# Making the inputs of a linear recurrence inside a top-k selection stage, per group of heads, and passing them through memory

## What is computed

```python
ps = p[..., :N_SHIFT]
ps = ps + (token_shift(ps) - ps) * shift_mu[l]
...
w_log = -jax.nn.softplus(-(w0 + jnp.tanh(pwd) @ w2).astype(f32)) - 0.5
decay = jnp.exp(-jnp.exp(w_log))
a = jax.nn.sigmoid((a0 + pad_ @ a2).astype(f32))
kk = heads(pk * k_k)
kk = kk / jnp.maximum(jnp.sqrt(jnp.sum(kk * kk, axis=-1, keepdims=True)), 1e-12)
k = pk.astype(f32) * (1.0 + (a - 1.0) * k_a)
...
y = rwkv7_scan(r_h, w_h, k_h, v_h, -kk, kk * a_h)
...
bonus = jnp.sum(r_h * k_h * r_k.astype(f32), axis=-1, keepdims=True) * v_h
```

## Time and profile before

| what | us |
| --- | --- |
| median of 3 runs (2827.34 to 2830.3) | 2829.26 |
| the profiled execution, its own time | 2830.62 |
| its span, first to last instruction | 2828.8 |
| TensorE busy in the span | 2563.4 (91%) |
| VectorE | 1502.1 (53%) |
| GpSimd | 901.7 (32%) |
| ScalarE | 784.5 (28%) |

### The profile page before, as it was taken

One profiled execution on the slowest core, in us unless ns is written; L12 is line 12 of the kernel. 1 busy time (PEld: TensorE's weight loads), 2 busy tenths in 40 slices (PEclk: granted clock), 3 DMA queues, 4 the chain that ended last, 5 costly groups with the idle time before them and its releaser, 6 DMA issues. The chain is left out here.

```text
span 2828.8 us, 40567 instructions
## 1 busy us (share of the span) xinstructions
PE 2563.4 (91%) x17201; PEld 2090.3 (74%) x17201; DVE 1502.1 (53%) x2111; ACT 784.5 (28%) x1334; POOL 901.7 (32%) x475
## 2 busy tenths in 40 slices
PE   7998899999999999989899999999898316899997
PEld 5887788888888888868675788887676106888686
DVE  5113633442422212234866899994565696555943
ACT  4205443310111101234424222211553311111332
POOL 3212333442433424444431122221310522111664
PEclk9999999999999999999999999999999658999999
DMA  3113212222221111122340133322100002100523
GB/s 132 40 37 121 74 45 104 68 80 90 80 90 63 45 45 52 45 82 75 102 152 30 60 105 90 105 89 78 64 1 21 14 30 77 33 4 9 197 91 109
DMA packets 76084, 200.06 MB, mean 71 GB/s; under 512 B 8408, under 2 KB 13056, under 8 KB 75904
## 3 DMA queue, kind: packets, MB, share of 16 engines
q1 hardware_dynamic: 65248, 178.06, 19.6%
q10 hardware_dynamic: 10656, 19.40, 1.8%
HBM read 166.88 MB, written 31.60 MB: 70 GB/s over the span
## 5 line engine op out<-in xcount | busy, mean ns | idle before, releaser
L339 PE MATMUL ps<-region_rounded,weights_hi_by_slot 128*128 128x512 f32 x2432 | 958.9, 394 | 32.9 <-DVE region_rounded L617 14.1
L340 PE MATMUL ps<-region_rounded,weights_hi_by_slot 128*128 128x512 f32 x2432 | 951.3, 391 | 0.0
L341 PE MATMUL ps<-region_rounded,weights_lo_in_place 128*128 128x512 f32 x2432 | 951.1, 391 | 0.0
L333 POOL TENSOR_TENSOR weights_lo_in_place<-wbuf,weights_hi_by_slot 128x1024 fp32r<-128x1024 f32 x194 | 486.2, 2509 | 933.9 <-ACT weights_hi_by_slot L329 933.9
L339 PEld LDWEIGHTS ps<-region_rounded,weights_hi_by_slot 128*128 128x128 f32 x2432 | 460.1, 189 | 135.0 <-issue 30.5
L340 PEld LDWEIGHTS ps<-region_rounded,weights_hi_by_slot 128*128 128x128 f32 x2432 | 459.8, 189 | 97.2 <-issue 2.6
L341 PEld LDWEIGHTS ps<-region_rounded,weights_lo_in_place 128*128 128x128 f32 x2432 | 459.4, 189 | 96.6
L329 ACT CAST weights_hi_by_slot<-wbuf 128x1024 fp32r<-128x1024 f32 x194 | 202.0, 1045 | 356.9 <-DMA wbuf<-w_mlp 218.9
L1819 DVE MAX8 gcols<-region 128x8 f32<-128x384 f32 (+5 forms) x192 | 171.7, 894 | 6.7 <-PEq L1708 0.3
L1821 DVE MATCH_REPLACE8 region<-gcols,region 128x384 f32<-128x384 f32 (+5 forms) x192 | 168.1, 876 | 0.0
L1529 DVE TENSOR_TENSOR region<-ps,region 128x512 f32<-128x512 f32 x64 | 44.1, 689 | 215.2 <-PE ps L341 215.1
(11 more groups left out here) (334 smaller groups left out, 3499.8 us busy)
## 6 DMA issues: line engine op xcount, KB each, us to landing
wbuf<-w_mlp SPq DMA_DIRECT2D x64, 512.0 KB, 3.6
wbuf<-w_hn SPq DMA_DIRECT2D x37, 512.0 KB, 4.7
scratch_hn_out<-tmp ACTq DMA_DIRECT2D x74, 256.0 KB, 4.8
region<-scratch_hn_out SPq DMA_DIRECT2D x37, 512.0 KB, 7.5
wbuf<-w_in SPq DMA_DIRECT2D x25, 512.0 KB, 3.7
region<-xT SPq DMA_DIRECT2D x24, 512.0 KB, 6.8
xtra<-w_ada SPq DMA_DIRECT2D x32, 384.0 KB, 4.2
wbuf<-w_att SPq DMA_DIRECT2D x20, 512.0 KB, 3.6
```

What stands on the lines that cost most here:

```text
L333: self.nc.gpsimd.tensor_tensor(self.m.lo4[:, n % SLOTS, :], self.m.raw4[:, n % SLOTS, :], self.m.hi4[:, n % SLOTS, :].bitcast(F32), ALU.su ...
L339: nc.tensor.matmul(out, m.hi4[:, s, w], m.rounded(hi + k, half(hf)), start=(k == 0), stop=False)
L340: nc.tensor.matmul(out, m.hi4[:, s, w], m.rounded(lo + k, half(hf)), start=False, stop=False)
L341: return nc.tensor.matmul(out, m.lo4[:, s, w], m.rounded(hi + k, half(hf)), start=False, stop=(k == KT - 1))
```

## The change

The selection stage's 37 units are put in another order (`HN_ORDER`): first the low rank unit (12), then for each group p its k, r and v unit and five other units, then the rest. So a group's period is 16 halves (`PERIOD`), and `group_at(j, first)` names the group whose step `first` falls on half j: j = 3 + first + 16p. At fixed steps each engine has a piece of one group's work behind its own:

- ScalarE drains a mixed unit twice per half, scaled by 1 - mu and by mu (the latter one column to the right, into xtra), and GpSimd adds the two (`mix`). That is the token mix.
- Step 0: k times k_k, its square (ScalarE). Step 1 and 3: low rank products, 128x512 in plain f32 (TensorE, banks 6 and 7), sigmoids (ScalarE). Step 1 also the head sums of the squares (TensorE, banks 4 and 5). Clamp on VectorE before round 22, 75, 117, 153 of its 192 (`CLAMP_AT`); square root at step 2 (ScalarE).
- Reciprocal, product, and 16 scans of 64 columns on VectorE before round 31, 81, 122, 158 (`INVERT_AT`).
- Step 5 and 6: factors (ScalarE), four products and one more (GpSimd); step 7: head sums of the bonus (TensorE); bonus products on VectorE before round 43, 91, 131, 165 (`BONUS_AT`); step 8: exponentials (ScalarE), products (GpSimd).
- SP stores the results to a new scratch in memory, `scan_in` (20 x 128 x 1024), and the bonus, between its weight loads.

Attention loads 12 of the 20 tiles at its start, and the 8 others (r and a), block of 128 columns by block, over the absorbed queries as these are used up. The five stages are gone. Semaphores are cleared by SP inside the index stage and attention; the block that cleared them on GpSimd is gone. The hn_out stores of 13 units are gone.

```diff
-def recycle_semaphores(nc):
-    with nc.Block() as block:
-        @block.gpsimd
-        def _(pool):
-            for s in IN_USE:
-                pool.sem_clear(s)
-    for s in IN_USE:
-        nc.release_semaphore(s)
+def retire_semaphores(m):
+    m.retired = list(IN_USE)
...
+            for sem in m.retired:
+                sp.sem_clear(sem)
...
+PERIOD = 16
+OTHERS = list(range(13, HN_UNITS))
+HN_ORDER = [12] + [n for p in range(RP) for n in [4 + p, p, 8 + p] + OTHERS[5 * p:5 * p + 5]] + OTHERS[5 * RP:]
 HN_FUNCS = [ACT.Identity] * 13 + [ACT.Silu] * 8 + [ACT.Sigmoid] * 16
+DECAY = float(np.exp(-0.5))
+PK, PR_, PKK, PA, PW_, PC = 28, 29, 30, 31, 33, 36
+CLAMP_AT, INVERT_AT, BONUS_AT = [22, 75, 117, 153], [31, 81, 122, 158], [43, 91, 131, 165]
+def group_at(j, first):
+    p, rest = divmod(j - 3 - first, PERIOD)
+    return p if rest == 0 and 0 <= p < RP else None
...
+    K, R, KK, A, W, C = [m.chunk(c) for c in (PK, PR_, PKK, PA, PW_, PC)]
+    X, LO, V = m.tflat[:, 2048:3072], m.tflat[:, 3072:4096], m.tflat[:, 1024:2048]
+    S1 = m.xtra[:, 0:T + 1]
+    lora_w = m.xtra[:, T + 32:T + 32 + 2 * P]
+    rest_mu, rest_ka = m.decay_b[:, 0:13], m.decay_b[:, 16:16 + RP]
+    mixes = [n for n in range(HN_UNITS) if HN_ORDER[n] < 13]
+    plain = [n for n in range(HN_UNITS) if HN_ORDER[n] >= 13]
+    def mixed(unit):
+        n = HN_ORDER.index(unit)
+        return mixes.index(n) + 1, [R, K, V, LO][unit // 4]
+    def key_mix(p):
+        return 3 * p + 2
...
+            load_lora(0)
+            for j in range(HALVES):
+                n = j // 2 + SLOTS
+                if j % 2 and n < HN_UNITS:
+                    st.load(sp, n, m.d["w_hn"][n])
+                p = group_at(j, 5)
+                if p is not None:
+                    sp.wait_ge(shifted, key_mix(p) + 2)
+                    sp.dma_start(m.d["scan_in"][12 + p], V).then_inc(v_stored, 16)
+                    if p + 1 < RP:
+                        load_lora(p + 1)
+                p = group_at(j, 7)
+                if p is not None:
+                    sp.wait_ge(ra_ready, p + 1)
+                    sp.dma_start(m.d["scan_in"][4 + p], W).then_inc(ra_stored, 16)
...
+            def mix(n):
+                q, dst = mixed(HN_ORDER[n])
+                pool.wait_ge(mixed_raw, 2 * q)
+                pool.wait_ge(taken, 2 * n + 2)
+                nc.gpsimd.tensor_tensor(dst, dst, S1[:, 0:T], ALU.add).then_inc(shifted, 1)
+            for j in range(HALVES):
+                n = j // 2
+                if j % 2 == 0 and n + 2 < HN_UNITS:
+                    st.lo(pool, n + 2)
+                if j % 2 and n in mixes:
+                    mix(n)
+                p = group_at(j, 5)
+                if p is not None:
+                    pool.wait_ge(cum_ready, NC * 2 * (p + 1))
+                    nc.gpsimd.tensor_tensor(W, C, W, ALU.subtract).then_inc(before_ready, 1)
+                    pool.wait_ge(factor_ready, p + 1)
+                    nc.gpsimd.tensor_tensor(K, K, X, ALU.mult).then_inc(k_ready, 1)
+                    pool.wait_ge(neg_ready, p + 1)
+                    nc.gpsimd.tensor_tensor(A, A, KK, ALU.mult).then_inc(b_ready, 1)
+                p = group_at(j, 6)
+                if p is not None:
+                    pool.wait_ge(rr_ready, p + 1)
+                    pool.wait_ge(k_ready, p + 1)
+                    nc.gpsimd.tensor_tensor(X, X, K, ALU.mult).then_inc(bonus_in, 1)
+                    pool.wait_ge(e1_ready, p + 1)
+                    nc.gpsimd.tensor_tensor(W, W, KK, ALU.mult).then_inc(ra_ready, 1)
+                p = group_at(j, 8)
+                if p is not None:
+                    pool.wait_ge(e2_ready, p + 1)
+                    nc.gpsimd.tensor_tensor(R, R, X, ALU.mult).then_inc(r_ready, 1)
+                    nc.gpsimd.tensor_copy(m.pl[:, p, :], X[:, RL - 1:T:RL]).then_inc(ends_ready, 1)
+                    pool.wait_ge(e3_ready, p + 1)
+                    nc.gpsimd.tensor_tensor(K, K, C, ALU.mult).then_inc(rk_ready, 1)
+                    pool.wait_ge(b_ready, p + 1)
+                    nc.gpsimd.tensor_tensor(A, A, C, ALU.mult).then_inc(rb_ready, 1)
         @block.tensor
         def _(pe):
-            for n in range(HN_UNITS):
+            def lora(p, q):
+                if p == 0:
+                    pe.wait_ge(tanh_done, 1)
+                pe.wait_ge(lora_loaded, 16 * (p + 1))
                 for hf in range(2):
-                    j = 2 * n + hf
-                    st.half_product(pe, n, j % 4, hf, NH, NL, taken, j - 3)
+                    if p or q == 0:
+                        pe.wait_ge(lora_taken, 4 * p + 2 * (1 - q))
+                    nc.tensor.matmul(m.ps[:, 6 + hf, :], lora_w[:, q * P:(q + 1) * P], LO[:, half(hf)],
+                                     start=True, stop=True).then_inc(lora_products, 1)
+            def head_sums(done):
+                for hf in range(2):
+                    nc.tensor.matmul(m.ps[:, 4 + hf, :], m.const("head_ones"), X[:, half(hf)], start=True, stop=True
+                                     ).then_inc(done, 1)
+            for j in range(HALVES):
+                st.half_product(pe, j // 2, j % 4, j % 2, NH, NL, taken, j - 3)
+                p = group_at(j, 1)
+                if p is not None:
+                    lora(p, 1)
+                    pe.wait_ge(squared, p + 1)
+                    if p:
+                        pe.wait_ge(bonus_out, 2 * p)
+                    head_sums(summed)
+                p = group_at(j, 3)
+                if p is not None:
+                    lora(p, 0)
+                p = group_at(j, 7)
+                if p is not None:
+                    pe.wait_ge(bonus_in, p + 1)
+                    pe.wait_ge(clamped, 2 * (p + 1))
+                    head_sums(bonus_summed)
...
+                nc.scalar.mul(dst[:, half(hf)], m.ps[:, j % 4, :], rest_mu[:, unit:unit + 1]).then_inc(mixed_raw, 1)
+                nc.scalar.mul(S1[:, 1 + hf * HALF:1 + (hf + 1) * HALF], m.ps[:, j % 4, :], m.par("mu", unit)).then_inc(taken, 1)
...
+                if j == 2:
+                    act.wait_ge(shifted, 1)
+                    nc.scalar.activation(LO[0:64], LO[0:64], ACT.Tanh).then_inc(tanh_done, 1)
+                p = group_at(j, 0)
+                if p is not None:
+                    act.wait_ge(shifted, key_mix(p))
+                    if p:
+                        act.wait_ge(rb_ready, p)
+                    nc.scalar.mul(KK, K, m.par("k_k", p)).then_inc(kk_raw, 1)
+                    act.wait_ge(kk_raw, p + 1)
+                    nc.scalar.activation(X, KK, ACT.Square).then_inc(squared, 1)
+                p = group_at(j, 1)
+                if p is not None:
+                    if p:
+                        act.wait_ge(rb_stored, 16 * p)
+                    lora_sigmoids(p, 1, A, "a0")
+                p = group_at(j, 2)
+                if p is not None:
+                    act.wait_ge(clamped, 2 * (p + 1))
+                    nc.scalar.activation(X, X, ACT.Sqrt).then_inc(rooted, 1)
+                p = group_at(j, 3)
+                if p is not None:
+                    if p:
+                        act.wait_ge(ra_stored, 16 * p)
+                    lora_sigmoids(p, 0, W, "w0")
+                p = group_at(j, 5)
+                if p is not None:
+                    act.wait_ge(kk_ready, p + 1)
+                    act.wait_ge(lora_taken, 4 * p + 2)
+                    nc.scalar.activation(X, A, ACT.Identity, bias=rest_ka[:, p:p + 1], scale=m.par("k_a", p)).then_inc(factor_ready, 1)
+                    act.wait_ge(factor_ready, p + 1)
+                    nc.scalar.mul(A, A, -1.0).then_inc(neg_ready, 1)
+                p = group_at(j, 6)
+                if p is not None:
+                    act.wait_ge(shifted, key_mix(p) + 1)
+                    act.wait_ge(k_ready, p + 1)
+                    nc.scalar.mul(X, R, m.par("r_k", p)).then_inc(rr_ready, 1)
+                    act.wait_ge(before_ready, p + 1)
+                    nc.scalar.activation(W, W, ACT.Exp, scale=-DECAY).then_inc(e1_ready, 1)
+                p = group_at(j, 8)
+                if p is not None:
+                    act.wait_ge(bonus_summed, 2 * (p + 1))
+                    act.wait_ge(before_ready, p + 1)
+                    nc.scalar.activation(X, C, ACT.Exp, scale=-DECAY).then_inc(e2_ready, 1)
+                    act.wait_ge(e2_ready, p + 1)
+                    nc.scalar.activation(C, C, ACT.Exp, scale=DECAY).then_inc(e3_ready, 1)
...
+            def clamp(p):
+                for hf in range(2):
+                    dve.wait_ge(summed, 2 * p + hf + 1)
+                    nc.vector.tensor_scalar(X[:, half(hf)], m.ps[:, 4 + hf, :], 1e-24, None, ALU.max).then_inc(clamped, 1)
+            def normalize_keys(p):
+                dve.wait_ge(rooted, p + 1)
+                for hf in range(2):
+                    nc.vector.reciprocal(X[:, half(hf)], X[:, half(hf)]).then_inc(inverse, 1)
```

(48 more changed lines are left out.)

304 lines of the change are left out of this document (80 added, 224 removed).

## The result

The changed kernel takes 2705.79 us (median of 4 runs, 2704.24 to 2707.20) against 2829.78 us of the kernel before (2827.34 to 2831.68): ratio 0.9562, 95% interval 0.9546 to 0.9579, 124 us less. The forecast was 2707 (2690 to 2731). The profiled execution took 2704.38 us with a span of 2702.6; the profiled one of before took 2830.62 with 2828.8.

The account below looks back on a forecast made before the run. TensorE was taken to bound the selection, and five uncovered small stages to stand in the chain. From 2830.6: -165.7 + 27.4 + 18 - 2 = 2708.3, less 1.4 for the median, so 2707 us; range 2690 to 2731.

Parts of the forecast that it names:

- What goes: Between attention and the recurrence: the five small stages and the semaphore clearing disappear, -166.0, or -165.7 with what stays.
- The plain seam of 0.3: Between attention and the recurrence: an ordinary gap between two stages remains, +0.3 us.
- TensorE's products: Selection: 32 added plain f32 matmuls at 0.86 us each, all on the path, +27.4 us.
- The waits: Selection: TensorE stalls for GpSimd's bonus product, 4.5 us a group, +18 us; bounds 10 and 20.
- The clock behind the waits: Selection: no term in the sum; TensorE's clock falling there was listed as a sign of a wrong prediction.
- VectorE: Selection: added clamps, reciprocals, products and scans come to 61 us, moving VectorE's end from 1943.1 to 2008.
- MAX8 beside GpSimd: Selection: GpSimd's time also excludes the top-k operations, the stage grows by 224, kernel 2886 us; chance 0.02.
- The groups run late: Selection: VectorE and TensorE wait for each other, stalls double to 36, plus 5 for attention's column load, 2730 us; chance 0.10.
- VectorE ends the stage: Selection: TensorE's wait is covered and VectorE finishes last at 2008, +31 in place of 45, 2692 us; chance 0.10.
- Attention: Attention: the column loads just fit before its end, 0 us, upper bound +5.
- The recurrence: Start of the recurrence: following straight behind matmuls it begins at a higher TensorE clock, -2 us, ends 0 and -4.
- ScalarE and SP: Selection: ScalarE's added activations and table loads, and SP's weight loads behind group waits, cost nothing.

Follow-up runs that it names:

- the kernel without waits: Against the changed kernel, ScalarE makes the inverse root as exp(-0.5 ln x), replacing its square root and VectorE's two reciprocals per group: 2689.43 us, ratio 0.9503.
- the first profiled execution: The changed kernel as first profiled, 2704.38 us; the one called second is the same kernel, unedited, run again in a later job, median 2709.88 us.

## Why the prediction was right, point by point

- **What goes** (-165.7): measured -165.7, from the same two ends. The plain seam of 0.3 was taken from the earlier trace rows and is 0.30.
- **TensorE's products** (+27.4; 32 x 0.86 is 27.5): 27.7 in the kernel without waits. Taking the pitch 0.86 rather than a duration was the right choice: the records say 592 ns, and two of them make one product.
- **The waits** (+18, bounds 10 and 20): 12.5 us, on the instruction and for the releaser named, and in all four groups: 2.14, 3.46, 3.20 and 3.68. The term was 5.5 too large. The exclusion that it was priced for is there (scans of 7.35, 7.41 and 5.2 us in three groups, the product at 2.52 in group 1), but the waits stayed near the lower bound, which was put in order without it. The second group, worked out in full there, came as it said: 3.46 for some 3, its bonus product ready at 1733.7 for 1733 to 1734 (in a stage that began 2.9 us earlier than before).
- **The clock behind the waits** was no term of the sum: the text only said that a falling clock would prove it wrong. The clock did fall, behind three of the four waits, so by that sign of its own the forecast failed on this step. It cost 5.8. Waits and clock together make 18.3 against +18. That is two errors of one size that cancel, which is luck, and the selection of the sum, 407.7 + 27.4 + 18 = 453.1 against 453.7, owes its closeness to that. (The "450 us" of the last paragraph was loosely put; its own two ends, 1568 and 2022, are 454 apart.)
- **VectorE** (+61): 66.0. Scans were priced at 0.28; free they go by at 0.19, under the lower bound of 0.21, and with the held ones they average 0.36 (23.0 / 64). The 5 us more are the exclusion, which the forecast had put in the waits and not in this sum. Not in the sum at all are the 4.5 us by which the old TENSOR_SCALAR grew. Its end was 2008, measured 2012.3 with an earlier start of the stage (1567.1 for 1570.0). TensorE ended 5.3 us behind it, within the 10 given.
- **MAX8 beside GpSimd** (the rival of 2886 us): 39.3 us for 32 of 1024 columns, as in the earlier trace rows, with GpSimd busy for 193 us; the 192 take 171.5 us. Refuted. The exclusion that the Trainium skill gives ("SBUF — State Buffer", section Who interferes with whom) holds where the forecast used it, for scans and for the two operand product (up to 2525 ns, 1225 alone), and leaves MAX8 free.
- **The groups run late** (2730) and **VectorE ends the stage** (2692): neither came in that form. The second was nearer the cause than its chance of 0.10 says: VectorE doesn't end the stage, but without the reciprocals the waits are gone. The text had VectorE's load as an alternative to the waits, where it is a part of their source.
- **Attention** (0, bound +5): 205.3 against 205.9, no late load.
- **The recurrence** (-2, 0 to -4): the part behind attention is 3.0 shorter in the first profiled execution and 0.2 shorter in the second. The mechanism exists; its yield is between 0 and 3, by the execution.
- **ScalarE and SP** at nothing: ScalarE is busy for 185 of 454 us, and TensorE's 15.7 idle us in the stage (453.7 less 438.05) are the 12.5 of waits and 3.2 at the end, for the last stores, as before.

The sum of 2708.3 for a profiled 2704.4 is off by 3.9: the selection came 0.6 us longer than in the sum, and attention 0.6, the recurrence 1.0 and the stages ahead of the selection 2.9 shorter.

## What to carry to other kernels

When work is moved under a stage, add it up for each engine there and ask which will be within a few per cent of the limit; the wait that shows up on TensorE may be named after GpSimd and begin with VectorE. Take load off the engine that starts the chain before you shorten the rest of it: moving two reciprocals to ScalarE's tables gave 18 us of the selection, reordering GpSimd 10, and both together no more than the first. Price waits of the matmul engine above their own length (here waits of 3.2 to 3.7 us cost 1.5 to 1.7 more in slow products, one of 2.14 us 0.1), and treat collisions of VectorE and GpSimd as a matter of phase, which has to be read again after each edit.

## What the runs showed of the hardware

- Behind waits of 3.2 to 3.7 us four records that take 1.88 us took 3.4 to 3.6; over 3 us behind one of these waits the granted clock was 0.69. Behind waits of 1.03 and 2.14 us they took 1.98, behind 2.24 us 2.93. Yet behind 2.80 us it was only 2.43, so the length of the wait alone doesn't set it.
- Scans of 64 columns follow each other every 0.19 us, and one held by GpSimd takes up to 2.49, about the length of a GpSimd product (2.4). How many are held depends on phase: 64 of them took 12.1, 18.6, 22.9, 23.0, 25.1 and 29.4 us in kernels that differ on other engines. A TENSOR_SCALAR of 512 columns took 2.38 us beside a GpSimd product and 0.43 without one.
- Two matmuls with 64 rows each in different rows of the array overlap: 1.06 us a pair in place of 1.71.
- The first 64 products of the recurrence took 2.59, 4.17 or 4.73 us behind the same 0.93 us gap, at a granted clock of 1.00, 0.59 and 0.50. Why the clock falls there in some executions and not in others was not found.
- Late and all together, loads ran at 399 and 411 GB/s in two windows of 4 us, with the 16 DMA engines' share at 1.0.
